# A 31-tap depthwise convolution on Trainium2: one of four channel chunks moved from VectorE to GpSimd, the other chunks' taps reordered

## The reference, cut to what matters

```python
def second_block(x, c, w_ada, ..., g_post):
    c_act = jax.nn.silu(c)
    for l in range(DEPTH):                       # DEPTH = 2
        mod = c_act @ w_ada[l] + b_ada[l]
        shift, scale, gate = jnp.split(mod, 3, axis=-1)
        h = rmsnorm_2(x, g_pre[l]) * (1.0 + scale[:, None, :]) + shift[:, None, :]
        p = h @ w_in[l]
        u_val, u_gate, g_conv, c_q, c_kv, k_idx, w_idx, g_attn = jnp.split(p, offsets, axis=-1)
        y_conv = conformer_conv(u_val, u_gate, conv_w[l], conv_b[l], ...) * jax.nn.silu(g_conv)
        y_attn = dsa_attention(c_q, c_kv, k_idx, w_idx, ...) * jax.nn.silu(g_attn)
        y = jnp.concatenate([y_conv, y_attn], axis=-1) @ w_out[l]
        x = x + gate[:, None, :] * rmsnorm_2(y, g_post[l])

def conformer_conv(u_val, u_gate, conv_w, conv_b, ln_g, ln_b, w_pw2):
    a = u_val * jax.nn.sigmoid(u_gate)
    # causal depthwise convolution over positions, 31 taps, 512 channels
    y = lax.conv_general_dilated(a, conv_w[:, None, :], window_strides=(1,), padding=[(30, 0)],
                                 feature_group_count=512) + conv_b
    y = jax.nn.silu(layernorm(y, ln_g, ln_b))
    return y @ w_pw2
```

## Time and profile before

| what | value |
|---|---|
| median of 3 runs | 950.68 us (950.64 to 950.72) |
| the profiled execution, its own time | 950.92 us |
| its span in the trace | 949.1 us |
| granted TensorE clock, mean | 0.999 of full speed |
| busy: PE, PEld | 936.4 us, 865.3 us |
| busy: DVE, ACT, POOL | 800.1 us, 278.1 us, 0.7 us |
| the taps (L2490), 240 instructions | 98.8 us busy |

### The profile page before, as it was taken

How to read it: one execution, slowest core, us unless ns; L and a number is a source line. 1 busy time by engine, 2 the same in 40 slices (tenths; PEclk the granted TensorE clock), 3 DMA queues, 4 the chain that set the end, 5 groups by cost and what they waited for, 6 DMA issues and landing times.

```text
span 949.1 us, 16131 instructions
## 1 busy us (share of the span) xinstructions
PE 936.4 (99%) x6456; PEld 865.3 (91%) x6456; DVE 800.1 (84%) x1822; ACT 278.1 (29%) x622; POOL 0.7 (0%) x7
## 2 busy tenths in 40 slices
PE   8999999999999999999999999999999999999997
PEld 7888999999999988889999999999888878888876
DVE  3778879999998878778699999988799985899953
ACT  1033122221212112263122221220424563624561
POOL 0000000000000000000000000000000000000000
PEclk9999999999999999999999999999999999999999
DMA  8943455464634750657254645447933428443101
GB/s 302 409 183 117 177 180 211 167 244 155 257 145 154 231 215 1 270 210 289 108 223 157 243 170 231 176 156 244 338 132 102 163 90 289 167 146 108 36 1 45
DMA packets 36859, 171.80 MB, mean 181 GB/s; under 512 B 5032, under 2 KB 8880, under 8 KB 23344
## 3 DMA queue, kind: packets, MB, share of 16 engines
q1 hardware_dynamic: 35120, 167.72, 48.0%
q10 hardware_dynamic: 1664, 3.04, 0.9%
HBM read 169.69 MB, written 2.64 MB: 182 GB/s over the span
## 4 chain that ended last, share of the span: by engine, by line
PE 92%; DVE 4%; DMA 2%; ACT 1%; issue 1%; ACTq 0%; SPq 0%; DVEq 0%
PE bank L1354 26%; PE bank L1374 14%; PE bank L1039 9%; PE bank L1457 5%; PE bank L1668 4%; PE bank L1107 3%; PE bank L1572 3%; PE bank L1330 3%; PE bank L1553 3%; PE bank L1300 3%; PE bank L1114 3%; PE bank L1654 3%; PE bank L1050 1%; PE bank L1497 1%; DMA ring<-in_ring 1%; PE bank L1600 1%
## 5 line engine op out<-in xcount | busy, mean ns | idle before, releaser
L1374 PE MATMUL bank<-work,fring 128*128 128x128 f32 x1008 | 115.5, 275 | 0.0
L1374 PEld LDWEIGHTS bank<-work,fring 128*128 128x128 f32 x1008 | 114.0, 192 | 0.0
L2490 DVE SCALAR_TENSOR_TENSOR work<-work,cols 128x256 f32<-128x256 f32 x240 | 98.8, 477 | 1.0 <-ACT work L893 0.5
L1354 PE MATMUL bank<-sq,fring 128*128 128x128 f32 x640 | 84.5, 275 | 0.0
L724 ACT ACTIVATE work<-work,cols 128x256 f32<-128x256 f32 x88 | 47.8, 593 | 110.8 <-DVE work L2213 96.0
L1354 PE MATMUL bank<-ring,fring 128*128 128x128 f32 x640 | 78.1, 275 | 0.0
L1354 PE MATMUL bank<-sq,ring 128*128 128x128 f32 x640 | 78.0, 275 | 0.0
L1354 PEld LDWEIGHTS bank<-sq,fring 128*128 128x128 f32 x640 | 77.9, 192 | 0.0
L1354 PEld LDWEIGHTS bank<-ring,fring 128*128 128x128 f32 x640 | 74.8, 192 | 0.2
L1354 PEld LDWEIGHTS bank<-sq,ring 128*128 128x128 f32 x640 | 74.7, 192 | 0.0
L2232 DVE SCALAR_TENSOR_TENSOR work<-work,cols 128x256 f32<-128x256 f32 x176 | 71.5, 477 | 0.0
(11 more groups left out here) (416 smaller groups left out, 1725.5 us busy)
## 6 DMA issues: line engine op xcount, KB each, us to landing
ring<-in_ring SPq DMA_DIRECT2D x60, 1024.0 KB, 6.9
fring<-in_up SPq DMA_DIRECT2D x44, 1024.0 KB, 6.9
ada_w<-in_ada SPq DMA_DIRECT2D x48, 512.0 KB, 6.3
fring<-in_down SPq DMA_DIRECT2D x44, 512.0 KB, 4.5
ring<-in_ring SPq DMA_DIRECT2D x2, 800.0 KB, 6.7
bias_skewed<-bias_rows SPq DMA_DIRECT2D x1, 1536.0 KB, 12.8
consts<-in_consts ACTq DMA_DIRECT2D x1, 1128.0 KB, 15.1
ring<-in_ring SPq DMA_DIRECT2D x2, 512.0 KB, 4.7
```

The source lines that it names most:

```text
L1354: last = mm(bank[:, P * at:P * (at + 1)], w[:, k, P * c:P * (c + 1)], x[:, k, :], start=(k == 0), stop=(k == 3))
L1374: last = mm(bank[:, at + P * c:at + P * (c + 1)], w[:, P * c:P * (c + 1)], x, start=(i == 0 and at == 0 and c == 0), stop=(i == FF_STEPS - 1),
L2490: marks[c] = link(v.scalar_tensor_tensor(b_y[:, c, :], b_a[:, c, tap:tap + T], col("conv_w_2", 124 * l + 4 * tap + c), b_y[:, c, :], ALU.m ...
```

## The change

The 30 taps of chunk 0 are taken from DVE and given to GpSimd in each layer. GpSimd has each tap as two instructions: a multiplication into the new tile `tap_out`, and an addition into `b_y[:, 0, :]`. Each waits by the semaphore `taps_step` for the one before it, and the first waits for ACT's tap 0 of chunk 0. DVE waits for the last of them before it adds the four chunks. DVE's remaining 90 taps per layer get new places: more of them, in chains of one chunk, before the index scores, and fewer between the heads. In heads 5 and 6 the reciprocal now comes ahead of the taps. Two DMA semaphores are merged into one (`row_in`), with the second waiter at 32.

```diff
+        tap_out = sb("tap_out", [P, T])
...
+            for l in range(DEPTH):
+                nc.gpsimd.wait_ge(S("conv0_done"), CC * l + 1)
+                for tap in range(1, TAPS):
+                    done = 2 * ((TAPS - 1) * l + tap - 1)
+                    if done > 0:
+                        nc.gpsimd.wait_ge(S("taps_step"), done)
+                    nc.gpsimd.tensor_scalar(tap_out[:, :], b_a[:, 0, tap:tap + T],
+                                            col("conv_w_2", 124 * l + 4 * tap), None, ALU.mult)\
+                        .then_inc(S("taps_step"), 1)
+                    nc.gpsimd.wait_ge(S("taps_step"), done + 1)
+                    nc.gpsimd.tensor_tensor(b_y[:, 0, :], b_y[:, 0, :], tap_out[:, :], ALU.add)\
+                        .then_inc(S("taps_step"), 1)
...
                 glu_raw(0)
                 normed(2, DC)
-                taps((0,), 4)
                 glu_raw(1)
-                taps((0, 1), 6)
+                taps((1,), 12)
...
-                taps((0, 1), 7)
+                taps((1,), 9)
                 mean_square(logs(l, CQ), pb[6][:, 0:T], ms[:, 0:T], 256)
...
                 ins.then_inc(S("cqn_done"), 1)
-                taps((0, 1), 7)
+                taps((1,), 9)
...
                 glu(2)
-                taps((0, 1, 2), 4)
-                taps((0, 2), 2)
-                taps((1, 2), 2)
+                taps((2,), 16)
                 glu(3)
...
-                taps((1, 3), 4)
-                taps((2, 3), 7)
-                taps((3,), 3)
+                taps((2, 3), 12)
...
                     if n_head == 0:
                         reciprocals(0)
-                        taps((2, 3), 1)
+                        taps((3,), 2)
                     elif n_head < 5:
-                        taps((2, 3), 2)
+                        taps((3,), 3)
...
                     elif n_head < 7:
                         if n_head == 6:
                             gate_attention(1)
-                        taps((2, 3), 2)
                         reciprocals(n_head)
-                        taps((2, 3), 1)
+                        taps((2,), 1)
+                        taps((3,), 2)
                     else:
-                        taps((3,), 1)
                         reciprocals(7)
+                        after(marks[2])
                         after(marks[3])
+                        dve.wait_ge(S("taps_step"), 2 * (TAPS - 1) * (l + 1))
                         then(v.tensor_tensor(b_ysq[:, 0:2, :], b_y[:, 0:2, :], b_y[:, 2:4, :], ALU.add))
...
-            sp.dma_start(gain_all, bass.AP(gain_row, 0, [[0, P], [1, D]])).then_inc(S("gain_in"), 16)
+            sp.dma_start(gain_all, bass.AP(gain_row, 0, [[0, P], [1, D]])).then_inc(S("row_in"), 16)
...
-                            dve.wait_ge(S("gain_in"), 16)
+                            dve.wait_ge(S("row_in"), 32)
```

More of the change, by code:

```diff
@@ L457, in _ @@
                 load(n)
-            sp.dma_start(c_row[:, :], I["c_2"][0].partition_broadcast(P)).then_inc(S("c_in"), 16)
+            sp.dma_start(c_row[:, :], I["c_2"][0].partition_broadcast(P)).then_inc(S("row_in"), 16)
             load_ada(0, 3)
@@ L735, in _ @@
             tables(SILU)
-            act.wait_ge(S("c_in"), 16)
+            act.wait_ge(S("row_in"), 16)
             nc.scalar.activation(c_row[:, :], c_row[:, :], ACT.Silu).then_inc(S("c_done"), 1)
@@ L2485, in taps @@
                             tap = done_taps[c] = done_taps[c] + 1
+                            assert c > 0
                             if tap == 1:
@@ L2641, in layer @@
                 gate_attention(2)
-                assert done_taps == [TAPS - 1] * CC
+                assert done_taps == [0] + [TAPS - 1] * 3, done_taps
                 dve.wait_ge(S("ss_done"), sums_on_pe(l, MEAN))
```

## The result

The changed kernel takes 976.11 us (median of 6 runs, 974.82 to 982.12) against 950.7 us before in the same comparison: a ratio of 1.0274, 95% interval 1.0255 to 1.0292. It is 25.4 us slower; 991 was forecast, with 949 to 1010 as the range. The profiled execution took 976.59 us, with a span of 974.8.

A forecast was written before the change was run, and what follows sets the result against it. PE bounds the kernel, 92% of the chain. DVE loses 23.2 us per layer to GpSimd, less 2.8 free, so PE loses 20.4; two layers add 40.8 to 950.9, 991 us after the median's 0.24; range 949 to 1010.

The forecast's parts named there:

- All that the change can win at PE: PE's idle time in and just behind the heads of both layers: together 1.5 us, were everything else free.
- The gain on DVE by `glu(3)`: Up to `glu(3)`, taps fall from 26.1 to 23.9 us, less 0.7 uncovered ahead of chunk 2: 1.5 us gained.
- The slack: DVE's permitted lateness before PE waits: 1.3 us at `glu(3)`, 0.8 us at head 0's transposes.
- The price on GpSimd: Per tap running alone: multiplication 0.31, addition 0.52, handovers 0.08, together 0.91 us, taken from memset rows.
- the sign that I had named: If the prediction is right, POOL finishes its taps 50 to 60 us behind tap 0.
- the upper end: DVE instructions reading two SBUF tensors stand for GpSimd's whole instruction: 0.85 x 27.3 = 23.2 us lost per layer.
- Where PE waits: Waits of about 10 us at `turn_kv` and the query projection's last quarter, each layer; nothing at the heads.
- No collision: Rival: GpSimd and DVE run side by side, PE wins at most 1.5 us, 949.2 to 950.7 us; chance 0.26.
- GpSimd last: Rival: at 3.5 us a tap DVE waits for GpSimd at the sum of chunks, 986 us or more; chance 0.06.
- the full collision: Likeliest case: DVE stands throughout GpSimd's instructions; 991 us, own range 976 to 1009; chance 0.54.
- the partial one: Rival: DVE slowed only part of the time, 0.3 us a tap, 961 us, from 953 to 976; chance 0.14.
- The clock: PE waits of 10 us may bring matmuls at 1.2 GHz behind them, 1 or 2 us each.

The follow-up runs named there:

- `mults_only`: The changed kernel with each GpSimd addition replaced by a second multiplication into `tap_out`: 963.47 us, ratio 1.0097 to 1.0135.

## Why the prediction was right, and what was mis-sized

*The bound.* "All that the change can win at PE" was put at 1.5 us; without GpSimd's taps the kernel is the same within 0.2%. Right.

*The gain on DVE by `glu(3)`, 1.5 us.* The prices of 0.52 and 0.40 us a step are right (16 taps took 8.30 us without GpSimd), as are the 0.7 us without cover. But the four taps taken from before `glu_raw(1)` were in the shadow of PE; DVE now waits there 1.8 us. It also waits 0.67 us for tap 0 of chunk 1 where it waited 0.27, and no longer the 0.79 us for ACT ahead of the first sum of squares. The gain was about nothing.

*The slack, 1.3 us at `glu(3)` and 0.8 at head 0.* Right. Counted from the block's start, `glu(3)` is (723.20 - 670.92) - (715.53 - 671.52) = 8.3 us late; less 1.3 that is 7.0, and PE's waits up to there are 1.4 at L1070 and 5.24, 6.6. The mask is 86.01 - 72.81 = 13.2 us late; less 0.8, plus 1.6 for the clock, 14.0, and the layer is 14.1 longer.

*The price on GpSimd, 0.91 us a tap.* Much too low: 0.98 + 0.84 us and gaps, 2.0 in all. A memset was a bad stand-in: it is 0.31 us at a size at which the multiplication is 0.97. So GpSimd did 30 taps in 59 us, not because it waited for DVE, as I had it, but nearly by itself: the sign that I had named, 50 to 60 us, came true for another reason.

*What it costs DVE* is the step that failed in size. I took the upper end, the whole of GpSimd's instructions for 85% of the time, 23.2 us a layer. It is 13.6 us a layer, 0.45 us a tap, 0.43 beside a single chain and (14.80 - 24 x 0.40) / 8 = 0.65 beside alternating ones, where eight GpSimd taps passed in the 14.8 us. Two things were wrong in the rule. VectorE is shut out for 0.26 + 0.53 = 0.79 us of a GpSimd tap and not for its 1.8; and of these 0.79 it meets only the part that is left when one of its instructions arrives, about half in single chains, whose taps start 0.22 and 0.30 us behind GpSimd's rows, and more in alternating ones, whose taps start 0.11 and 0.06 behind them. Had I priced GpSimd right and kept my rule of whole instructions, the error would have been larger: 30 x 1.8 x 0.85 = 46 us a layer. My 0.31 and 0.52 us, meant as GpSimd's durations, happen to be close to the times for which it shuts VectorE out. The two errors partly cancelled, and that the measured time lies so near the forecast is to this extent luck.

*Where PE waits.* At `glu(3)`, right, 5.2 and 5.4 us instead of 10. At `turn_kv` not at all: DVE's scale ended at 711.78, PE came at 712.64. And at the heads, where I had said nothing would show, 3.3 and 1.7 us: GpSimd was still at work until 739, beside DVE's 24 alternating taps behind `glu(3)`.

*The rivals.* No collision is excluded by the taps of 0.84 us. GpSimd last: it ended at 739 us, DVE's sum of chunks came at 781.85. The measured case is between the two: VectorE stands still, as in the full collision, but only for the first part of an instruction, which is nearer to the partial one, and the size is nearly that one's too: 976 is the border that I had put between them. The clock, kept for the upper end, was there but mostly off the path.

## What to carry to other kernels

Before work is moved off a busy engine, ask whether the time can come back at the engine that bounds the kernel: here at most 1.5 us could, and the move cost 25. Elementwise work on GpSimd isn't free beside VectorE work that reads two SBUF tensors: it cost 0.45 us of VectorE per tap, more than the 0.40 us that the same tap cost VectorE itself. Beside the picking (MAX8 and MATCH_REPLACE8, one tensor each) it cost nothing. A single SBUF input is no safe sign, though: the TENSOR_SCALAR of 128x16 at L2547 has one and took 0.70 us instead of 0.17.

## What the runs showed of the hardware that was not expected

- On GpSimd a 128x256 multiplication by a column took 0.92 us with no collision and the addition of two tiles 0.73, so the one with fewer inputs is the slower; over 128 columns they averaged 0.67 and 0.49.
- GpSimd's instructions shut VectorE out only for their first part: 0.26 us of 0.92 for the multiplication, 0.53 of 0.73 for the addition, 0.26 of 0.46 for the addition over 128 columns. Whoever starts behind it waits to the same moment.
- Between the same two engines the price depends on the rhythm: a multiplication cost a tap 0.10 us beside a single chain and 0.21 beside alternating ones, an addition 0.34 and 0.47.
- A TENSOR_SCALAR with one SBUF input was held as well: 0.70 us instead of 0.17 over 128x16, and, in `mults_only`, 0.37 instead of 0.16 over 128x2.
- VectorE held GpSimd for less: beside single chains the multiplication went from 0.92 to 0.97 us and the addition from 0.73 to 0.85; in `mults_only` the multiplication went to 1.04.
